# Token modulation, splitting and the first projections done group by group, behind column groups of the modulation weights

## The reference, cut to what matters

```python
def modulation(cvec, w_ada, b_ada):
    m = jnp.matmul(jax.nn.silu(cvec), w_ada) + b_ada      # 2048 -> 6 * 2048
    return jnp.split(m[..., None, :], N_MOD, axis=-1)

sh1, sc1, g1, sh2, sc2, g2 = modulation(c, ada_w[l], ada_b[l])
csh1, csc1, ... = modulation(c_ctx, ada_w[l], ada_b[l])
zl = jnp.matmul(xl * (1.0 + sc1) + sh1, w_in[l])          # 512 latent tokens
zc = jnp.matmul(xc * (1.0 + csc1) + csh1, w_in[l])        # 256 context tokens
...                                                       # mixers, output projection, MLP
```

## Time and profile before

| | |
|---|---|
| Median of 3 timed runs | 3180.15 us (3172.73 to 3182.63) |
| Profiled execution, its own time | 3187.81 us |
| Its span | 3186.0 us |
| PE busy | 2948.1 us (93%) |
| DVE busy | 1478.7 us (46%) |
| POOL busy | 1135.3 us (36%) |
| ACT busy | 686.0 us (22%) |
| Mean granted TensorE clock | 0.959 of full |
| Data moved by DMA | 398.57 MB |

### The profile page before, as it was taken

One profiled execution on the slowest core, in us unless ns is written; L12 is line 12 of the kernel. 1 busy time (PEld: TensorE's weight loads), 2 busy tenths in 40 slices (PEclk: granted clock), 3 DMA queues, 4 the chain that ended last, 5 costly groups with the idle time before them and its releaser, 6 DMA issues.

```text
span 3186.0 us, 59462 instructions
## 1 busy us (share of the span) xinstructions
PE 2948.1 (93%) x24772; PEld 2420.3 (76%) x24772; DVE 1478.7 (46%) x1845; ACT 686.0 (22%) x1013; POOL 1135.3 (36%) x674
## 2 busy tenths in 40 slices
PE   5799998899998489999998999999999999999996
PEld 0577886687777489988786888888888888888885
DVE  0676677444866534444425433333333343333336
ACT  0222222102222112122113212122221212122221
POOL 0343343434342112210343444444444444444442
PEclk7799998899999799999999999999999999999998
DMA  9675566532433432223432332332332233233322
GB/s 402 237 242 179 193 216 214 178 79 65 156 104 126 150 80 66 67 71 107 185 94 66 93 99 93 94 99 93 94 98 93 93 98 95 93 96 96 94 93 112
DMA packets 164890, 398.57 MB, mean 125 GB/s; under 512 B 73952, under 2 KB 78048, under 8 KB 157856
## 3 DMA queue, kind: packets, MB, share of 16 engines
q1 hardware_dynamic: 134016, 296.00, 28.9%
q10 hardware_dynamic: 30336, 96.64, 8.7%
q0 software_dynamic: 288, 2.10, 0.2%
HBM read 358.89 MB, written 35.80 MB: 124 GB/s over the span
## 4 chain that ended last, share of the span: by engine, by line
PE 62%; DVE 2%; issue 1%; DMA 0%; ACT 0%; POOL 0%; POOLq 0%; SPq 0%; DVEq 0%; ACTq 0%
PE bank L1062 17%; PE bank L1063 16%; PE bank L1061 16%; PE bank L784 7%; PE bank L800 2%; PE bank L872 1%; PE bank L946 1%; PE bank L944 1%; PE bank L860 1%; DVE buf L1928 0%; DVE buf L1929 0%; PE bank L808 0%; DMA buf<-lnrows 0%; DVE buf L1885 0%; DMA buf<-scaled_keys 0%
## 5 line engine op out<-in xcount | busy, mean ns | idle before, releaser
L627 POOL TENSOR_TENSOR buf<-buf 128x1024 fp32r<-128x1024 f32 x288 | 697.7, 2423 | 1015.9 <-ACT buf L1261 1015.9
L1062 PE MATMUL bank<-buf 128*128 128x512 f32 x2304 | 909.0, 395 | 0.0
L1063 PE MATMUL bank<-buf 128*128 128x512 f32 x2304 | 908.1, 394 | 0.0
L1061 PE MATMUL bank<-buf 128*128 128x512 f32 x2304 | 904.5, 393 | 0.5 <-POOL buf L627 0.4
L1261 ACT CAST buf<-buf 128x1024 fp32r<-128x1024 f32 x288 | 303.4, 1053 | 1262.7 <-PE bank L1063 1261.4
L1061 PEld LDWEIGHTS bank<-buf 128*128 128x128 f32 x2304 | 433.1, 188 | 104.7 <-issue 2.8
L1062 PEld LDWEIGHTS bank<-buf 128*128 128x128 f32 x2304 | 432.4, 188 | 101.6 <-issue 0.5
L1063 PEld LDWEIGHTS bank<-buf 128*128 128x128 f32 x2304 | 432.5, 188 | 96.8
L651 PE MATMUL bank<-buf 128*128 128x512 f32 (+1 forms) x1168 | 431.3, 369 | 20.4 <-POOL buf L594 11.8
L652 PE MATMUL bank<-buf 128*128 128x512 f32 (+1 forms) x1168 | 422.9, 362 | 0.0
L653 PE MATMUL bank<-buf 128*128 128x512 f32 (+1 forms) x1168 | 418.1, 358 | 0.0
(11 more groups left out here) (222 smaller groups left out, 2214.8 us busy)
## 6 DMA issues: line engine op xcount, KB each, us to landing
buf<-stream SPq DMA_DIRECT2D x382, 512.0 KB, 3.6
buf<-adarows ACTq DMA_DIRECT2D x108, 512.0 KB, 4.9
buf<-ada SPq DMA_DIRECT2D x32, 1024.0 KB, 13.1
scaled_keys<-buf ACTq DMA_DIRECT2D x18, 768.0 KB, 5.7
buf<-scaled_keys SPq DMA_DIRECT2D x18, 768.0 KB, 6.7
buf<-adarows SPq DMA_DIRECT2D x20, 512.0 KB, 6.9
buf<-tokens SPq DMA_DIRECT2D x4, 1536.0 KB, 21.2
buf<-bias ACTq DMA_DIRECT2D x6, 1024.0 KB, 6.4
```

The costliest lines, as they stand in the source:

```text
L627: G.tensor_tensor(wl2[b % SPLIT2], raw2[b], wh2[b % SPLIT2].bitcast(F32), ALU.subtract).then_inc(split2, 1)
L1061: pe.matmul(bank[:, :], lh, rh, start=start, stop=False)
L1062: pe.matmul(bank[:, :], lh, rl, start=False, stop=False)
L1063: return pe.matmul(bank[:, :], ll, rh, start=False, stop=stop)
```

## The change

The weights of shift and scale are laid out in four column groups. Group q holds, for shift and for scale, columns 512q to 512q+511 of all 2048 input rows, in eight tiles of 1 MB; a tile is now four k-tiles of 512 columns, of one vector. The order is: group, then vector, then k. Each tile still gives four matmuls of 128 x 2 by 128 x 512, but all four are terms of one sum and write the same two rows, partitions 0 and 1 of bank 5 (shift) or bank 6 (scale).

After each group its rows are copied (ACT), turned (eight tiny matmuls into bank 7, behind the second tile of the next group), and bias and 1.0 are added (DVE); then its four token k-tiles are modulated and split. The token buffer holds one group instead of four, and its loads move to ACT's list: group 0 at the start, group q+1 when group q is split. The first six pieces of projection weights are reordered (first halves of tiles 0, 1, 2, then second halves) and are loaded among the `ada` tiles. From tile 12 of the `ada` loop on, TensorE does one step of the first three projections behind each tile, all of group 0's k-tiles for the three tiles, then group 1's, and so on; what is left after the last tile is done at its end.

The diff, cut to its core (renumbered waits on `mod_ev` and `v_mod` and the unchanged rest are left out):

```diff
+FIRST_TILES, ROWS_BANK, TURNED_BANK, QUARTER_BEHIND = 3, 5, 7, 12
+FIRST_PIECES = {10: (0, 1), 14: (2,), 16: (3,), 18: (4,), 31: (5,)}
...
-        xraw = take(KT * TOK, F32, phase).rearrange("p (k t) -> p k t", k=KT)
+        xraw = take(4 * TOK, F32, phase).rearrange("p (k t) -> p k t", k=4)
...
-            for b in range(RING0):
-                sp.dma_start(ring0[b], ada[b]).then_inc(loaded0[b], 16)
-            for i in range(RING0, 2 * KT):
-                sp.wait_ge(used_pe, i - RING0 + 1)
+            def piece(n):
+                if n >= RINGW:
+                    sp.wait_ge(split, n - RINGW + 1)
+                sp.dma_start(raw[n % RINGW], stream1[n]).then_inc(rawld[n % RINGW], 16)
+
+            for i in range(2 * KT):
+                for n in FIRST_PIECES.get(i, ()):
+                    piece(n)
+                if i >= RING0:
+                    sp.wait_ge(used_pe, i - RING0 + 1)
                 sp.dma_start(ring0[i % RING0], ada[i]).then_inc(loaded0[i % RING0], 16)
-            for q in range(4):
-                sp.dma_start(xraw[:, 4 * q:4 * q + 4, :], tokens[q]).then_inc(xld[q], 16)
-            for b in range(RINGW):
-                sp.dma_start(raw[b], stream1[b]).then_inc(rawld[b], 16)
-            early = {0: 2, RINGR: 1, RINGR + 2: 1, RINGR + 7: 1, RINGR + 12: 1}
-            pieces = RINGW
+            early = {0: 2, RINGR + 7: 1, RINGR + 12: 1}
+            pieces = 2 * FIRST_TILES
...
+        def first_projections(pe):
+            for q in range(4):
+                for n in range(FIRST_TILES):
+                    if q % 2 == 0:
+                        pe.wait_ge(split, FIRST_TILES * (q // 2) + n + 1)
+                    for part, (bank, _, _) in enumerate(TILES[n]):
+                        width, cols = (SEQ, lat) if part == 0 else (CTX, slice(0, CTX))
+                        per = 2 + 2 * part
+                        for k in range(4 * q, 4 * q + 4):
+                            if n == 0 and part == 0:
+                                pe.wait_ge(xsplit, k + 1)
...                          # the three matmuls of L651 to L653, from wh[n], wl[n]
+                            if part == len(TILES[n]) - 1 and k % 8 == 7:
+                                mm.then_inc(used1, 1)
+                            if k % per == per - 1:
+                                yield
...
+            def turn_rows(q):
+                pe.wait_ge(rows_copied, 2 * q + 2)
+                for c in range(2):
+                    for k in range(4):
+                        at = 16 * q + 8 * c + 2 * k
+                        mm = pe.matmul(banks[TURNED_BANK][:, at:at + 2],
+                                       rowb[0:2, 512 * c + P * k:512 * c + P * k + P], ident[0:2, 0:2], start=True, stop=True)
                 mm.then_inc(rows_turned, 1)
-
+            first = first_projections(pe)
             for i in range(2 * KT):
-                (c, k), b = divmod(i, KT), i % RING0
+                (q, rest), b = divmod(i, 8), i % RING0
+                c, group = divmod(rest, 4)
                 pe.wait_ge(loaded0[b], 16 * (i // RING0) + 16)
-                for q in range(4):
-                    mm = pe.matmul(banks[4 * c + q][32 * q:32 * q + 2, :], csil[:, k, :], ring0[b][:, 512 * q:512 * q + 512],
+                if q and group == 0:
+                    pe.wait_ge(rows_copied, 2 * q - 1 + c)
+                for u in range(4):
+                    k = 4 * group + u
+                    mm = pe.matmul(banks[ROWS_BANK + c][0:2, :], csil[:, k, :], ring0[b][:, 512 * u:512 * u + 512],
                                    start=k == 0, stop=k == KT - 1)
                 mm.then_inc(used_pe, 1)
-                if i == KT + 3:
-                    turn_rows(0)
-            turn_rows(1)
-            pe.wait_ge(mod_ev, 2)
-            finish(projection(pe, range(3)))
+                if i >= 9 and i % 8 == 1:
+                    turn_rows(i // 8 - 1)
+                if i >= QUARTER_BEHIND:
+                    next(first)
+            turn_rows(3)
+            finish(first)
...
+            act.dma_start(xraw, tokens[0]).then_inc(xld[0], 16)
+            for q in range(4):
+                for c in range(2):
+                    act.wait_ge(used_pe, 8 * q + 4 * c + 4)
+                    nc.scalar.copy(rowb[0:2, 512 * c:512 * c + 512], banks[ROWS_BANK + c][0:2, :]).then_inc(rows_copied, 1)
+                act.wait_ge(v_mod, q + 1)
+                act.wait_ge(xld[q], 16)
...                          # modulate k-tiles 4q to 4q+3, as L1473 and L1474
+                if q < 3:
+                    act.wait_ge(xsplit, 4 * q + 4)
+                    act.dma_start(xraw, tokens[q + 1]).then_inc(xld[q + 1], 16)
...
+    stream1[0:6] = stream1[[0, 2, 4, 1, 3, 5]]
-    ada, adarows = vectors[0:2].reshape(2 * KT, P, D), vectors[2:].reshape(4 * KT, P, D)
+    ada = vectors[0:2].reshape(2, 4, 4, P, 4, 512).transpose(4, 0, 1, 3, 2, 5).reshape(2 * KT, P, D)
```

## The result

| | before | after |
|---|---|---|
| Median of the timed runs | 3180.15 us | 3210.7 us (3203.77 to 3216.05) |
| Ratio to before, 95% interval | | 1.0095 (1.0076 to 1.0113) |
| Span of the profiled execution | 3186.0 us | 3208.8 us |
| PE busy | 2948.1 us | 3012.0 us |
| Mean granted TensorE clock | 0.959 | 0.967 |

The account below looks back on a forecast made before the run. Stage 1, bound by loading before, becomes bound by TensorE: last tile at 159.8 us, last token split 169.9, half rows done at 202 instead of 176, so +26 on 3180.15 gives 3206 us; range 3186 to 3223.

Parts of the forecast that it names:

- A tile's price: Stage 1 on TensorE: eight passes in one strip do not overlap, 3.44 us a tile, 2.4 us more than before.
- (a): Stage 1: loading still bounds it, DVE starts pair 0 25 us earlier than before, 3155 us; chance 0.07.
- (c): Stage 1: passes in one strip overlap in part, a tile costs 2.5 us, 3176 us; chance 0.03.
- Rival (b): Sums serialise, but half rows are fast and the last tile early: +9 us or less, 3189 us; chance 0.08.
- The clock rival (d): Stage 1: clock stays at half while only two columns work; twelve unwoven tiles add 38 us, 3244 us; chance 0.07.
- start, tokens beside it, first tile slow: Start of stage 1: 8.4 us start, 1.5 for group 0's tokens on another queue, 2.5 for first tiles at half clock.
- woven steps before the last tile: Twenty projection steps between stage 1's tiles: 28.0 us at 1.4 each, plus 5.6 for switching matmul forms.
- three `turn_rows`: Turning on TensorE before the last tile's end: 16 passes each, 3.7 us in all, or 6.8 at the slower price.
- The switch between the two forms of matmul: TensorE going from two-column float32 to full form and back at each woven step: 0.28 us, 5.6 for twenty.
- All waits costed at nothing: Stage 1's new waits (copied rows, group turning and splits, piece 3, token loads): no cost, covered by TensorE's 4.8 us a tile.
- the stretch of the first 16 half rows: SP's queue and DVE, between last token split and pair 0's attention: 32 us, ends 26 and 36.5, finishing at 202.
- the forecast of +26 us: DVE starts pair 0's attention at 202 instead of 176, and the kernel's end is 26 us late; chance 0.75.

Follow-up runs that it names:

- the kernel with four strips: Changed kernel with a tile's four matmuls put back into four strips of output partitions, summed by the turning matmul: 3156.65 us, ratio 0.9924.
- The short half rows: Changed kernel loading and summing only 128 of 1024 columns of half rows 2 to 15: 3195.5 us, ratio 1.0054.
- before, one strip: Kernel before, with a tile's four matmuls writing partitions 0 and 1 of their four banks instead of four strips: 3207.66 us, ratio 1.0093.
- four strips, no weaving: Changed kernel with four strips, all 32 steps of the first three projections after the last tile: 3170.25 us, ratio 0.9965.
- no weaving, rows among pieces: Four strips without weaving, pieces 5 to 7 loaded among the half rows, which wait for the last weight tile: 3173.27 us, ratio 0.9973.
- four strips, rows behind last tile: Changed kernel with four strips, first four half rows waiting for the last weight tile instead of the last token split: 3147.31 us, ratio 0.9898.
- four strips, short half rows: Changed kernel with four strips, only 128 of 1024 columns of half rows 2 to 15 loaded and summed: 3140.75 us, ratio 0.9877.

## Why the prediction was right

**The root.** A tile's price was the step on which everything stood: eight passes at 0.43 us in one strip, 3.44 us, against 1.04 in four. Measured 3.45, in *after* and, alone, in the kernel before. The row that gave the 0.43 is of passes that write all 128 partitions (`128*128`); that passes with two output rows in one strip stand as far apart was inferred from it, and it held. The rival of a stage still bound by loads (a) is out, and so is (c), for which a tile would have had to take 2.5 us. By the figure for column strips in the Trainium skill (TensorE: Matmul & The Clock Gate, Measured speedup vs the span model), going back to one strip would cost a factor of 2.38 for three strips; for the four strips here it is 3.45 / 1.04 = 3.3. Rival (b), an early last tile and fast half rows, is out with 159.5 and a stretch of 35.6 us. The clock rival (d) is out too: the granted clock is 1.00 from 10 to 126 us, with TensorE busy nearly all the time, most of it on two-column matmuls.

**The last tile.** Forecast 159.8, measured 159.5. The mechanism is right; that the number is so close is partly luck, since four terms were off and cancel:

| term | forecast | measured |
|---|---|---|
| start, tokens beside it, first tile slow | 12.4 | 10.2 (second tile at 13.68, less 3.45) |
| 32 tiles | 32 x 3.44 = 110.1 | 32 x 3.45 = 110.4 |
| woven steps before the last tile | 20 x 1.68 = 33.6 | 19 x 1.66 = 31.5 |
| three `turn_rows` | 3.7 | 3 x 1.9 = 5.7 |
| clock at half for a while | 0 | 1.6 |
| sum | 159.8 | 159.4 |

The steps were counted wrong: each step comes behind its tile, so the step of tile 31 comes after the last tile, and 19 lie before it. The turning was priced at half of 2.47 us, but that row is of passes that read from four strips of input partitions, while the changed kernel reads all rows from one (the last section has the comparison). And the clock fell once: it was at 0.50 from about 128 to 131 us, right behind the third `turn_rows`, although TensorE had been busy without a gap since 13.68. The window (columns as in the earlier trace rows) and TensorE's timeline:

```profile
126.00:136.00 10.00, 10.00 (x40) 5.09 (x40) 7.22 (x9) 4.90 (x8) 3.98 (x2) 0.83 0.44 145
```

```profile
129.43 4.52 PE L1158 MATMUL bank<-buf 128*2 128x512 f32 x8
```

The switch between the two forms of matmul, taken from the nearest row with a price of 0.28 us for there and back, is 5.10 - 3.44 - 1.4 = 0.26. The tokens on the second queue show in the kernel with four strips: its second tile comes at 13.56, not at 10.8, and the third at 16.5. In *after* the slow first tile (5.47 us) covers that. I call it a tile at half clock by the length of its passes; the clock in the window from 0 to 10 us reads 1.00.

**Behind it.** The last token split was to come at 169.9, 10.1 us behind the last tile, and came at 170.8, 11.3 us behind it: the step of tile 31 stands ahead of the turning, and the turning took 1.9 us instead of 1.25. Tile 2 was to be 13.2 us late and was 14.6 late. All waits costed at nothing cost nothing: in the first 180 us TensorE waits for `ada` alone.

**The term that was mis-sized** is the stretch of the first 16 half rows: 32 us, measured 206.4 - 170.8 = 35.6, nearly the upper end, 36.5. I had let two pieces and a split that fall out of the stretch save 4.8 us. Two pieces did fall out, but the bias table was now asked for 9 us into the stretch, at 180.2, where before that was 3 us ahead of its end, and the DMA engines moved 11.2 MB in it as before (314 GB/s over 35.6 us, 307 over 36.5). No split fell out: three lie in it before and after. VectorE's waits for loads grew from 10.7 to 11.7 us in sum, and its sums took 1.8 us less. That is most of the difference between the forecast of +26 us and the 30 us measured: VectorE starts pair 0 30.4 us late instead of 26.

**Who passes it on.** That the lateness goes through the half rows and VectorE, and not through TensorE's 13 us, was argued from order and from a wait of 2.3 us. The short half rows show it for 13 of the 30 us. Over all kernels that were tried, the shifts against the kernel before are these, in us (tile 2 is taken by ScalarE when TensorE has ended it; ScalarE starts pair 1 when it is through with pair 0):

| kernel | tile 2 taken, against 165.7 | VectorE starts pair 0, against 176.0 | ScalarE starts pair 1, against 230.8 | time |
|---|---|---|---|---|
| changed kernel | +14.6 | +30.4 | +28.3 | +30 |
| before, one strip | +27.3 | +25.6 | +26.2 | +30 |
| changed, short half rows | +14.1 | +18.0 | +13.8 | +17 |
| four strips, no weaving | -5.9 | -4.2 | -8.6 | -11 |
| no weaving, rows among pieces | -6.1 | -7.0 | -8.9 | -9 |
| four strips | -35.9 | -19.3 | -21.3 | -24 |
| four strips, rows behind last tile | -35.8 | -24.9 | -27.6 | -32 |
| four strips, short half rows | -36.0 | -32.0 | -37.1 | -39 |

In the changed kernel VectorE is 16 us later than TensorE, TensorE waits 10.1 us for it, and the time follows VectorE. In the last three rows TensorE is 36 us early each time, and the time moves with VectorE's start. In the kernel before with one strip and in the two kernels without weaving the two engines are shifted nearly alike, so these rows do not tell them apart. That the later of the two sets the end fits all rows to within 7 us.

The faster kernels gain 2 to 7 us more than VectorE's earlier start; 2 to 5 us of that is there when ScalarE starts pair 1, and I have not shown its cause. One recorded execution can't settle a few microseconds at the end of 3200: the shift of *after* against before is 28 us at the end of pair 0 and 22.8 at the end of the two recorded spans, while the timed runs say 30. The recorded execution of the kernel before was 7.7 us above its median, that of *after* at its median, which is the difference.

## What to carry to other kernels

Matmuls with few output rows were cheap here only side by side. Before regrouping sums, look at the output partitions of consecutive matmuls: if a tile's four matmuls take about as long as one alone (1.04 us against 1.02 here), they overlap, and writing them to one strip multiplies their price (3.45). Keep the strips as partial sums and add them later. Here the matmul that turned the rows anyway did the sum over four strips, for 1.8 us more of copying on ScalarE for each vector and group, and it turned a loss of 30 us into a gain of 24.

When a stage moves, follow the queue behind its last semaphore. A wait that was merely convenient (the half rows behind the last token split, where the last weight tile is enough) was worth some 8 us more once it lay on the path.

## What the runs showed of the hardware that I had not expected

- Reading from one strip of input partitions has a price too. The 32 turning passes behind the twentieth tile take 2.47 us in the kernel before, where the rows lie in four strips, and 3.73 in the kernel before with one strip, both at a granted clock of 1.00 and into the same banks. The 16 passes of *after* take 1.94 us, the same 0.12 a pass.
- Neighbouring passes in one strip stay 0.43 us apart even when they write four different banks (kernel before with one strip: 3.45 us for eight).
- The granted clock fell to 0.50 from about 128 to 131 us of *after*, in the middle of more than 100 us in which TensorE was never idle; the tile in it took 4.52 us instead of 3.60. What brought it down, the runs do not show.
- A 1.5 MB load on a second queue put the second 1 MB tile back by 2.7 us (13.56 against 10.8) and the third by 3.2 (16.51 against 13.3), so it gets its share at once and is not served behind the tiles.
